# Experts in 64-row blocks with native fp32 products in two column halves, eight weight slots and rows selected on chip

## What is computed

```python
g_logits = hf @ w_rg + b_rg                     # 4 groups, the best one is taken
e_logits = (hf @ w_re + b_re)[group]            # 8 experts in a group, the best two
top_w = softmax(top_val) * p_grp
# the 1024 pairs (token, expert) are sorted by expert, in blocks of one expert
def expert_block(xblk, e):
    return (silu(xblk @ w_gate[e]) * (xblk @ w_up[e])) @ w_down[e]
out[token] += weight * y[row of the pair]
```

## Time and profile before

| | |
|---|---|
| median of 3 runs | 2031.33 us (2028.53 to 2032.62) |
| profiled execution | 2027.54 us, its span 2026.0 us |
| PE busy | 1887.8 us, 93% of the span |
| DVE, ACT, POOL busy | 1240.0, 1010.1, 117.3 us |
| mean granted PE clock | 0.970 |
| expert weights | 96 transfers of 2048 KB |
| routing | from about 245 to 334 us of the span |
| experts | from about 340 to 920 us |
| combine and projection | from about 920 us |

### The profile page before, as it was taken

How to read it: one execution, slowest core, us unless ns; L and a number is a source line. 1 busy time by engine, 2 the same in 40 slices (tenths; PEclk the granted TensorE clock), 3 DMA queues, 4 the chain that set the end, 5 groups by cost and what they waited for, 6 DMA issues and landing times. The chain is left out here.

```text
span 2026.0 us, 28669 instructions
## 1 busy us (share of the span) xinstructions
PE 1887.8 (93%) x10664; PEld 1545.2 (76%) x10664; DVE 1240.0 (61%) x1677; ACT 1010.1 (50%) x1461; POOL 117.3 (6%) x161
## 2 busy tenths in 40 slices
PE   6999896999999999992999989899999989999997
PEld 3873444888888888872975479889999779999886
DVE  4855665899999999987236546634235454444433
ACT  4323413888888888875356643345332333232322
POOL 1001001111111111101100000000000000000000
PEclk9999997999999999995989989999999999999999
DMA  9837814999999999995211011112323113323321
GB/s 369 281 124 264 331 55 167 356 384 386 388 391 384 385 390 382 388 338 181 63 32 42 0 43 43 43 42 86 103 84 114 53 53 104 100 88 94 115 83 42
DMA packets 116230, 373.21 MB, mean 184 GB/s; under 512 B 8175, under 2 KB 70917, under 8 KB 102823
## 3 DMA queue, kind: packets, MB, share of 16 engines
q1 hardware_dynamic: 108566, 348.08, 47.0%
q0 software_dynamic: 7200, 23.66, 3.5%
q10 hardware_dynamic: 370, 0.14, 0.0%
HBM read 333.62 MB, written 33.82 MB: 181 GB/s over the span
## 5 line engine op out<-in xcount | busy, mean ns | idle before, releaser
L1480 DVE TENSOR_TENSOR parts_memory<-fixed,parts_memory 128x1024 fp32r<-128x1024 f32 x384 | 443.0, 1219 | 50.4 <-ACT parts_memory L1430 48.4
L1430 ACT ACTIVATE parts_memory<-fixed 128x1024 fp32r<-128x1024 f32 x384 | 375.2, 1066 | 28.9 <-DMA fixed<-in_w_exp_gate_dram 17.7
L1695 PE MATMUL psum<-parts_memory 128*128 128x256 f32 (+3 forms) x1136 | 346.9, 305 | 9.5 <-PEq L1909 3.3
L1696 PE MATMUL psum<-parts_memory 128*128 128x256 f32 (+3 forms) x1136 | 343.7, 303 | 0.0
L1697 PE MATMUL psum<-parts_memory 128*128 128x256 f32 (+3 forms) x1136 | 343.2, 302 | 0.0
L1594 DVE TENSOR_TENSOR parts_memory<-fixed,parts_memory 128x1024 fp32r<-128x1024 f32 x139 | 166.8, 1221 | 220.4 <-ACT parts_memory L1586 220.4
L1695 PEld LDWEIGHTS psum<-parts_memory 128*128 128x128 f32 x1136 | 218.5, 192 | 19.2 <-DVE parts_memory L1594 4.6
L1697 PEld LDWEIGHTS psum<-parts_memory 128*128 128x128 f32 x1136 | 218.4, 192 | 6.9
L1696 PEld LDWEIGHTS psum<-parts_memory 128*128 128x128 f32 x1136 | 218.1, 192 | 7.0
L1695 PE MATMUL psum<-mix_parts,parts_memory 128*128 128x256 f32 (+2 forms) x664 | 206.2, 310 | 4.7 <-PEq L2613 4.0
L1696 PE MATMUL psum<-mix_parts,parts_memory 128*128 128x256 f32 (+2 forms) x664 | 207.2, 312 | 0.0
(11 more groups left out here) (425 smaller groups left out, 2901.7 us busy)
## 6 DMA issues: line engine op xcount, KB each, us to landing
fixed<-in_w_exp_down_dram SPq DMA_DIRECT2D x32, 2048.0 KB, 9.9
fixed<-in_w_exp_gate_dram SPq DMA_DIRECT2D x32, 2048.0 KB
fixed<-in_w_exp_up_dram SPq DMA_DIRECT2D x32, 2048.0 KB, 10.5
fixed<-in_w_in_dram SPq DMA_DIRECT2D x36, 1024.0 KB, 5.6
expert_rows<-fixed SPq DMA_DIRECT2D x8, 2560.0 KB, 25.4
fixed<-in_w_mod_dram SPq DMA_DIRECT2D x8, 2048.0 KB, 9.1
fixed<-in_w_ffn_up_dram SPq DMA_DIRECT2D x11, 1024.0 KB, 5.4
fixed<-in_w_ffn_gate_dram SPq DMA_DIRECT2D x11, 1024.0 KB, 5.4
```

The costliest lines, as they stand in the source:

```text
L1430: act.activation(weights[:, 0, piece, :], ring[:, s, q * PIECE:(q + 1) * PIECE], ACT.Copy).then_inc(high_ok, 1)
L1480: dve.tensor_tensor(out, src, high_part.bitcast(F32), ALU.subtract).then_inc(done, 1)
L1695: pe.matmul(out, x(0), w(0), start=start, stop=False)
L1696: pe.matmul(out, x(0), w(1), start=False, stop=False)
```

## The change

- Blocks have 64 rows (`BR`). Each of the 32 experts has one base block, written out without a loop and with its number known beforehand; every further 64 rows of an expert are an extra block in a loop of 15 rounds at the end, whose number is read from `more`.
- No weight, row or hidden value is split. `select` makes the block's rows from `h2`, which stays in SBUF: DVE compares each pair's row number with the block's 64 places (`choice`), and PE multiplies the one-hot matrix with `h2`. All products are native fp32 with 64 stationary columns; the left half of the result's columns goes to partitions 0 to 63 and the right half to 64 to 127.
- PE's order in a base block is gate(b), up(b), `select(b+1)`, `turn_h(b)`, `turn_x(b+1)`, down(b). ACT copies the selected and the transposed rows and takes silu; DVE makes the hidden rows, the one-hots of block b+2, the copy of the hidden rows and the copy of the result.
- Eight slots for weights (the old ring and memory of the first block that is no longer in use). SP loads into a slot as soon as PE has read it.
- Routing is in the same `Block` as the experts, so the barrier between them is gone, and so are the stores of `h2` to DRAM, all gathers of rows, the one-hot tables and their products. `idle_products` are four after the output products (new) and four after the ranks (three and three before).
- POOL stores a block's result in two halves of 64 rows x 2 KB. Only the extra blocks' rows are zeroed beforehand, 4 MB in two stores.

```diff
+BR = 64
+MORE = 16
+BLOCKS = EXPERTS + MORE
-ZERO_STORES = 8
-HALF_BLOCK = P // 2
+ZERO_STORES = 2
@@ route_sync
+        for i in range(3):
+            load_expert(g, sp, i)
+        for i, (sem, count) in enumerate(((ready, 2 * TT - 1), (ready, 2 * TT), (ready, 2 * TT), (h2s, 2 * TT), (r_ps, TT)), 3):
+            sp.wait_ge(sem, count)
+            load_expert(g, sp, i)
@@ route_dve, after the ranks
+        step(dve.tensor_scalar(counted, psum[:, 7, P:P + EXPERTS], 31.5 - BR, BIG, ALU.add, ALU.add))
...
+        choose_rows()
@@ experts, sync
+            for i in range(EXPERT_SLOTS, LOADS):
+                sp.wait_ge(w_read, i - EXPERT_SLOTS + 1)
+                load_expert(g, sp, i)
+            n = blocks_more(sp)
+            with sp.If(0 < n):
+                load_more(0, LOADS - EXPERT_SLOTS + 1)
@@ experts, gpsimd
+            def store(b, j):
+                pool.wait_ge(y_sb, b + 1)
+                for h in range(2):
+                    pool.dma_start(dram["y"].rearrange("(b r) n -> r b n", r=BR)[:, bass.ds(b, 1), 512 * h:512 * h + 512],
+                                   yb[j][half(h), :].unsqueeze(1)).then_inc(y_st[j], 16)
@@ experts, tensor
+            def select(b):
...
+                for t in range(TT):
+                    for h in range(2):
+                        last = pe.matmul(psum[half(h), BX, :], pick[:, j, t, :], h2[:, t, 512 * h:512 * h + 512],
+                                         start=(t == 0), stop=(t == TT - 1))
+            def project(bank, slot, arrived):
+                pe.wait_ge(w_in[slot], arrived)
...
+                for k in range(KT):
+                    x = xT[:, (k % 4) * P + (k // 4) * BR:(k % 4) * P + (k // 4) * BR + BR]
+                    for h in range(2):
+                        last = pe.matmul(psum[half(h), bank, 0:256], x, w[:, k, 256 * h:256 * h + 256],
+                                         start=(k == 0), stop=(k == KT - 1))
+            def turn_h(b):
...
+                for q in range(4):
+                    for h in range(2):
+                        last = pe.matmul(psum[half(h), BH, q * BR:(q + 1) * BR], hb[half(h), q * BR:(q + 1) * BR],
+                                         ident[half(h), half(h)], start=True, stop=True)
+            for b in range(EXPERTS):
+                where = [(i % EXPERT_SLOTS, 16 * (i // EXPERT_SLOTS + 1)) for i in range(3 * b, 3 * b + 3)]
+                gate_and_up(b, where)
+                if b + 1 < EXPERTS:
+                    select(b + 1)
+                turn_h(b)
+                if b + 1 < EXPERTS:
+                    turn_x(b + 1)
+                down(b, *where[2])
+            loop(pe, blocks_more(pe), more_rows)
@@ experts, vector
+            for b in range(EXPERTS):
+                hidden(b)
+                if b + 2 < EXPERTS:
+                    choose_rows(b + 2)
+                take_h(b)
+                take_y(b)
```

More of the change, by code:

```diff
@@ L1305, in _ @@
+            combine_sync(sp)
         @block.gpsimd
         def _(pool):
[L1307 to L1318 removed]
@@ L1354, in _ @@
+            for b in range(EXPERTS):
+                store(b, b % Y_SLOTS)
+            n = blocks_more(pool)
+            loop(pool, n, lambda i: store(i + EXPERTS, 0))
+            pool.wait_ge(y_st[0], n * 32 + 32 * EXPERTS // Y_SLOTS)
+            for j in range(1, Y_SLOTS):
+                pool.wait_ge(y_st[j], 32 * EXPERTS // Y_SLOTS)
+            pool.sem_inc(seen, 1)
             combine_pool(pool)
@@ new lines, in down @@
+            def down(b, slot, arrived):
+                pe.wait_ge(ht_ok, b + 1)
+                wait(pe, y_sb, b)
+                pe.wait_ge(w_in[slot], arrived)
+                w = slots[slot].rearrange("p (k n) -> p k n", k=4)
+                for q in range(4):
+                    for h in range(2):
+                        last = pe.matmul(psum[half(h), BY, :], hT[:, q * BR:(q + 1) * BR], w[:, q, 512 * h:512 * h + 512],
+                                         start=(q == 0), stop=(q == 3))
+                last.then_inc(w_read, 1)
@@ L1418, in _, with more_rows @@
-            turn_h(n * 2 - 1, 1)
-            down(n * 2 - 1, 1, last_down_at, n * 2)
+                project(BU, *where[1])
+            def more_rows(i):
+                b = i + EXPERTS
+                where = [(kind, i * 16 + 16 * (LOADS // EXPERT_SLOTS + 1)) for kind in range(3)]
+                select(b)
+                turn_x(b)
+                gate_and_up(b, where)
+                turn_h(b)
+                down(b, *where[2])
+            route_pe(pe)
+            select(0)
+            turn_x(0)
@@ L1475, in _ @@
+            route_act(act)
+            take_rows(0)
+            take_x(0)
+            for b in range(EXPERTS):
+                gate(b)
+                if b + 1 < EXPERTS:
+                    take_rows(b + 1)
+                    take_x(b + 1)
+            n = blocks_more(act)
+            loop(act, n, more_rows)
+            act.wait_ge(w_read, n * 3 + LOADS)
             combine_act(act)
@@ L1521, in _ @@
+            loop(dve, n, more_rows)
             combine_dve(dve)
```

895 lines of the change are left out of this document (370 added, 525 removed).

## The result

The changed kernel takes 1954.28 us (median of 4 runs, 1952.22 to 1957.48), the kernel before beside it 2031.97 us (4 runs). The ratio is **0.9621**, with a 95% interval of 0.9603 to 0.9640. The profiled execution took 1952.22 us with a span of 1950.6 us, 75.3 us less than the one of before. The forecast was 1967, with 1952 to 1994 as its range; the median measured lies 2.3 us inside its lower end.

The account below looks back on a forecast made before the run. PE was taken to pace the expert stage, DMA close behind. Start 333, 31 blocks of 15.5, last block 12.6, extra block 25 and tail 19.6 put the first mix at 870.7, gain 63.6: 1967 us, range 1952 to 1994.

Parts of the forecast that it names:

- PE for one block: Expert stage: PE paces at 15.5 us a block, bounds 15.2 and 15.9, with column halves running together.
- DMA for one block: Expert stage: weights at 420 GB/s plus the result store take 16.3 or 17.6 us a block.
- rival 1: Expert stage: DMA paces instead of PE, 1981 us taken, 1998 at 17.6 us a block; chance 0.22.
- The cover by the eight slots: Expert stage: loads issued ahead cover slower DMA, so PE paces; break-even at 16.5 us a block of DMA.
- The start: Routing to first gate: gate(0) at about 333 us, before 347.58; 3 us later if filler products fail.
- the prediction's own sign of being wrong: Stated failure test: a block period above 16 us, or routing ending later than before.
- The extra block: Loop after the base blocks: exactly one 33rd block, 22 us plus about 3 for lowered clock: 25, bounds 20 and 30.
- The tail: Last down to first mix: 19.6 us through DVE with 14 empty rounds at 0.68; POOL's gather needs 16.
- Behind the first mix: Everything after the first mix: unchanged code, so its time was taken as unchanged.
- 2: Whole kernel: less than summed, turns hidden (15.2 us a block), extra work 20, no clock lost: 1953 us; chance 0.09.
- 3: Expert products: column halves overlap only partly, gain gone at 17.55 us a block; chance 0.07 with anything else slower.
- 4: Extra-block loop: more extra blocks than one, 20 us each, three for no gain; no separate chance given.

Follow-up runs that it names:

- the short selection: Changed kernel with row selection over one token tile in place of four, 6 of 8 products left out per block: 1936.06 us.
- four slots: Changed kernel with four expert weight slots in place of eight: 1959.35 us, ratio 0.9656 to the kernel before.
- the run with both engines relieved: Changed kernel with row selection over one token tile and, from the ninth load on, half the bytes per expert weight load: 1866.84 us.
- two of the gaps filled: Changed kernel with idle products before the first h2 transposes and the ranks, and empty extra-block rounds skipped: 1943.88 us, ratio 0.9589.
- the halved weights: Changed kernel fetching half the bytes of each expert weight load from the ninth on, same TensorE work: 1954.83 us.
- the halves apart: Changed kernel with select, gate, up and down running all products of the first column half, then all of the second: 2144.31 us.

## Why the prediction was right, and where it was not

- **PE for one block: right.** 15.28 us lie within 15.2 to 15.9. The four products take 3.45, 3.46, 3.53 and 3.48 us from start to start, 13.9 in sum (13.8 predicted from the earlier trace rows); the turns 1.36 (0.77 and 0.59) in place of 1.7, and no idle time stands before either. They hold all small products and the three changes of layout together.
- **DMA for one block: mis-sized.** 16.3 us were predicted, 17.6 as the other end; DMA alone needs about 15.3 (the short selection). The 420 GB/s of the earlier trace rows came from a window of 4.7 us; over the stage it is 427. And the store was priced at half of the 2.6 us that gather and store cost together; at the rate of the stage its 0.26 MB are 0.6 us. So the picture of a slower DMA that the head start just covers was wrong: DMA was never behind. That its period and PE's came out equal is chance; no term of the forecast says so. The weight of 0.22 for rival 1 rested on this term.
- **The cover by the eight slots: right in kind.** It was to hold while DMA needs up to 16.5 us a block. The short selection shows the head start being used up, at 2.58 us a block in nine blocks, and four slots show that with equal periods it is hardly called on.
- **The start: the step that failed.** The idle products were to hold the clock up: they did for the last transposes (1.32 us against 1.78), but the clock fell earlier, at 247 and 274 us, and again ahead of the ranks, where no filler stood. It cost 6.4 us, more than the 3 allowed. The ranks start at 326.27 us, 3.5 later than in the kernel before, so by them the prediction's own sign of being wrong, that routing ends later than before, did come. The step still gains because from there to the first gate there are 13.1 us where before there were 24.8: the gather and the barrier are gone. Where the clock held, the step's numbers come out: in the run with both engines relieved, at full clock until 319 us, the rank products start at 321.07 (320.9 forecast), and with two of the gaps filled gate(0) is at 333.67 (333).
- **The extra block: right but for the clock.** 21.5 us against 22 without the 3 for a lowered clock. The clock stayed at 1.00, where before the products behind the gap ran at half; in the profile of four slots it did fall there, and the block took 22.8.
- **The tail: mis-sized, and by another path.** An empty round costs DVE 0.50 us, not 0.68, the distance of two starts in the earlier trace rows; 14 of them give 2.5 us less. The forecast took DVE as the last to be ready (19.6 us) and POOL's gather as ready after 16; the gather was the last, at 17.9, with ACT idle for 1.52 us on it.
- **Behind the first mix: "everything behind is unchanged code" was right, and the time changed all the same**, by 6.0 us that go with clock falls.
- **Rivals.** 1 did not come, by the runs with the short selection and the halved weights. 2 is close to what was measured (1953, 15.2 us a block), but by other terms. 3 names the right point: one order of the very same instructions is 2144 us, slower than before, and one placement 2184. What it rested on, an overlap lost evenly in all pairs, is not what happens: alternating pairs lose nothing that can be seen. The Trainium skill's 2.38 times for three column tiles (TensorE: Matmul & The Clock Gate, Measured speedup vs the span model) has no counterpart here: two halves give 6.91 / 3.45 = 2.00. 4 did not come: one extra block.

Taken one by one the steps are off by 24.6 us, in sum by 11.7, since the start came late and the others early. That the total came out inside the range owes something to luck: with the start at 333 us, as forecast and as two filled gaps give it, about 6 us less would have lain below the range.

## What to carry to other kernels

Products with 64 stationary columns in different column halves of the array gave two for one here, as long as their order in the program alternated in short chunks; write the loop over the halves inside the loop over the contraction. When two engines both look full, take work from each in turn: here both had 15.3 us, so neither alone could give more than its head start. Skip a run-time loop's empty rounds at once. And look at the granted clock of unchanged stages before a difference of a few us is put down to an edit.

## What was not expected of the hardware

- PE starts products out of the program's order across column halves, about four records (two fp32 products) ahead: in the profile of the halves apart, gate's records start at 613.68 with three records of `down` still to start.
- Full halves of fp32 products overlap without loss: 0.216 us for a pair, 0.432 in one half.
- The granted clock falls to half (1.2 GHz), in routing for 3.4 to 13.7 us at a time, and for other times and at other places in other executions of unchanged code: behind the first mix 64.6 to 81.5 us in sum, which went with up to 6.7 us of time.
- The mean rate of the DMA engines over 400 us, with PE full, was 427 GB/s, at 2 MB a load and 128 KB stores among them.
